# A fused mixer block on one NeuronCore: the six middle blocks of each engine's program become the body of a counted loop

## The reference

```python
mod = silu(c) @ w_ada + b_ada;  shift, scale, gate = split(mod, 3)
h = rms_norm(x, norm_g) * (1 + scale) + shift
proj = h @ w_in                      # 4096 x 1024 @ 1024 x 3592
pool_out = causal_pool_mixer(u) * silu(z_pool)      # windows 2, 4, 8, 16
q, k = silu(causal_depthwise_conv(proj[q, k]))
hm = mlstm_chunkwise(q, k, v, ig, lf)               # chunks of 128, 4 heads, state carried
mlstm_out = rms_norm_heads(hm) * mh_norm_g * sigmoid(o) * silu(z_mlstm)
x = x + gate * (concat(pool_out, mlstm_out) @ w_out)
out = rms_norm(x, final_g)
```

## Time and profile before

| what | value |
|---|---|
| median of 3 runs | 1903.21 us (1901.49 to 1903.31) |
| the profiled execution | 1901.49 us, its span 1899.7 us |
| PE busy | 1815.9 us, 96% of the span, 9505 matmuls |
| DVE busy | 1081.1 us, 57%, 2453 instructions |
| ACT, POOL busy | 470.0 us (25%), 238.1 us (13%) |
| TensorE's granted clock | 0.994 of full speed over the span |
| DMA | 324 MB, 171 GB/s; the 16 DMA engines 51% busy with it |
| code fetched during the run | 1.25 MB in 76 packets (queue 8), 0.35 MB in 43 (queue 14) |

### The profile page before, as it was taken

The page is one execution under the profiler, slowest core; times in us unless marked ns, Lnnn a source line. Parts: engine busy times, 40 slices in busy tenths (PEclk is TensorE's granted clock), DMA queues, the critical chain, the costliest instruction groups (busy, mean ns, idle before and its releaser), DMA issues.

```text
span 1899.7 us, 25000 instructions
## 1 busy us (share of the span) xinstructions
PE 1815.9 (96%) x9505; PEld 1551.8 (82%) x9505; DVE 1081.1 (57%) x2453; ACT 470.0 (25%) x970; POOL 238.1 (13%) x213
## 2 busy tenths in 40 slices
PE   2797999999999999999999999999999999999998
PEld 1686878988888888988889888888889888898886
DVE  7677585454746366372764637544573727636373
ACT  1134432212312122221222122221221212222221
POOL 0443213000120002200030000300012000210000
PEclk9998999999999999999999999999999999999999
DMA  9597952665235652456425663265524564255521
GB/s 298 174 307 261 308 182 78 203 196 200 90 135 191 207 176 80 157 189 210 152 74 186 189 203 119 89 210 189 195 72 164 188 211 150 87 171 193 169 100 67
DMA packets 131483, 324.12 MB, mean 171 GB/s; under 512 B 11724, under 2 KB 49316, under 8 KB 131364
## 3 DMA queue, kind: packets, MB, share of 16 engines
q1 hardware_dynamic: 131364, 322.53, 51.4%
HBM read 276.28 MB, written 46.20 MB: 170 GB/s over the span
## 4 chain that ended last, share of the span: by engine, by line
PE 77%; DVE 11%; DMA 4%; issue 2%; POOL 1%; ACT 1%; SPq 0%; DVEq 0%; POOLq 0%
PE ps_acc L466 21%; PE ps_acc L468 21%; PE ps_acc L467 20%; DMA w_kept<-sb_w_split 3%; DMA sb_w_raw<-w_in 2%; PE ps_kv L466 1%; PE ps_kv L467 1%; PE ps_kv L468 1%; PE ps_num L479 1%; PE ps_sco L625 1%; DVE sb_shifted L1429 1%; DVE sb_acc_cv L1429 1%; PE ps_num L653 1%; PE ps_kv L657 1%; PE ps_num L652 1%
## 5 line engine op out<-in xcount | busy, mean ns | idle before, releaser
L466 PE MATMUL ps_acc<-sb_hT_hi,sb_w_split 128*128 128x512 f32 x1536 | 603.3, 393 | 0.0
L468 PE MATMUL ps_acc<-sb_hT_hi,sb_w_split 128*128 128x512 f32 x1536 | 599.3, 390 | 0.0
L467 PE MATMUL ps_acc<-sb_hT_lo,sb_w_split 128*128 128x512 f32 x1536 | 599.1, 390 | 0.0
L468 PEld LDWEIGHTS ps_acc<-sb_hT_hi,sb_w_split 128*128 128x128 f32 x1536 | 288.8, 188 | 61.4
L467 PEld LDWEIGHTS ps_acc<-sb_hT_lo,sb_w_split 128*128 128x128 f32 x1536 | 289.1, 188 | 59.3
L466 PEld LDWEIGHTS ps_acc<-sb_hT_hi,sb_w_split 128*128 128x128 f32 x1536 | 289.4, 188 | 57.9
L971 POOL TENSOR_TENSOR sb_h_rs<-sb_h_var,sb_mhalf 128x4 f32<-128x4 f32 x32 | 32.4, 1014 | 1118.1 <-DVE sb_h_var L1380 1118.1
L1291 DVE SCALAR_TENSOR_TENSOR sb_acc_cv<-sb_shifted,sb_par,sb_acc_cv 128x512 f32<-128x512 f32 x192 | 146.2, 761 | 6.8
L1314 DVE TENSOR_TENSOR sb_oz<-sb_tanh,sb_oz 128x512 f32<-128x512 f32 x32 | 22.2, 692 | 147.0 <-ACT sb_tanh L855 147.0
L466 PE MATMUL ps_acc<-sb_wo_hi,sb_mixm_hi 128*128 128x512 f32 x256 | 103.9, 406 | 0.0
L468 PE MATMUL ps_acc<-sb_wo_hi,sb_mixm_lo 128*128 128x512 f32 x256 | 100.1, 391 | 0.0
(11 more groups left out here) (220 smaller groups left out, 2884.2 us busy)
## 6 DMA issues: line engine op xcount, KB each, us to landing
sb_w_split<-w_kept SPq DMA_DIRECT2D x344, 512.0 KB, 3.6
sb_w_split<-w_kept SPq DMA_DIRECT2D x56, 520.0 KB, 4.1
w_kept<-sb_w_split SPq DMA_DIRECT2D x40, 512.0 KB, 5.8
sb_x_res<-x SPq DMA_DIRECT2D x34, 512.0 KB, 4.5
out<-sb_x_res SPq DMA_DIRECT2D x32, 512.0 KB, 2.6
sb_x_in<-x SPq DMA_DIRECT2D x30, 512.0 KB, 5.3
sb_w_raw<-w_in SPq DMA_DIRECT2D x48, 256.0 KB, 4.4
w_kept<-sb_w_split SPq DMA_DIRECT2D x8, 520.0 KB, 4.7
```

Source lines behind the costliest of these rows:

```text
L466: pe.matmul(dst, st_hi, mv_hi, start=start, stop=False)
L467: pe.matmul(dst, st_hi, mv_lo, start=False, stop=False)
L468: return pe.matmul(dst, st_lo, mv_hi, start=False, stop=stop)
```

## The change

In each of the five engine functions the Python `for` over blocks 1 to 6 is replaced with a counted loop of the engine (`Fori`). The program of an engine then holds the middle block once; `b` is a register of that engine, each wait whose value hangs on `b` is for the content of a register that the sequencer works out, and the addresses of `x` and `out` are made from `b` too. Blocks 0 and 7 stay as they were, outside the loop. The loops of the five engines are separate, with no barrier at their ends.

```diff
@@ block.sync @@
             one_block(0, False, True)
-            for b in range(1, NB - 1):
+            with sp.Fori(1, NB - 1) as b:
                 one_block(b, False)
             one_block(NB - 1, True)
@@ block.tensor @@
-            for b in range(1, NB - 1):
+            with pe.Fori(1, NB - 1) as b:
@@ block.scalar @@
-            for b in range(1, NB - 1):
+            with act.Fori(1, NB - 1) as b:
@@ block.gpsimd @@
-            for b in range(1, NB - 1):
+            with pool.Fori(1, NB - 1) as b:
@@ block.vector @@
-            for b in range(1, NB - 1):
+            with dve.Fori(1, NB - 1) as b:
```

## The result

| kernel | median | runs | ratio to before |
|---|---|---|---|
| before (measured again beside it) | 1903.26 us | 1900.66 to 1904.02, six | |
| after, five counted loops | 1919.01 us | 1917.57 to 1919.97, six | 1.0085, 95% interval 1.0075 to 1.0096 |

The loops cost 15.8 us, 0.85%. The forecast was slower, 1914 us, 10.6 us for the change: the direction and the range held, the size was a third too small. That the sum was of the right order is largely luck, since its parts were not: in the profiled execution the jumps cost 7.4 us and not 10, and not by the packet of code that the 10 stood for, and the register instructions inside the blocks 6.8 us and not 0.6.

What follows compares the result with a forecast made beforehand. PE's stream was taken to bound every middle block. Jumps at 10 us plus 0.6 us of register work, on 1901.5, gave 1912.1; set 1.7 us higher for the median, 1914 us, own range 1907 to 1921, with rivals 1901 to 1930.

Steps and rivals of the forecast that it cites:

- the register instructions inside the blocks: Register work in the middle blocks: nothing on DVE, 0.1 us at PE's wait of line 479, six times, 0.6 us.
- The period that it named: From the second middle block on, each block would take 226 us, against 223.9 before.
- the second packet: PE code needed ten matmuls past each jump back: there at 7.2 us, PE dry from 5.3; five times, 10 us.
- F: Time to fetch the target's code again at a jump back, taken as 3.6 us, between bounds of 1.2 and 5.1.
- its signs: Expected in the profile: PE idle about 2 us ten matmuls into five blocks; idle at the first matmul means larger F or C.
- The register instruction between two dependent steps: On DVE it runs while the first step is being executed, so it was costed at nothing.
- Rival D: Register work shows on DVE's chain to the head output: 2.7 us a block, 16 us in six, 1919 us; 12%.
- The 0.6 us for PE's own register instruction at line 479: The wait for DVE's head output sits on a sequencer instruction ahead of the matmul: 0.1 us, six times.
- The forecast of 0 for SP, ACT and POOL: Their jumps cost nothing: SP's late load is hidden by PE's own 2.0 us, ACT's fetch lies in its wait, POOL is idle.
- B: The code fetch hides at the jumps and costs PE nothing; 1904 us; 27%.
- C: The sequencer doesn't jump before PE's queue is empty: 6.3 us, five times, 31 us, 1934 us; 10%.
- E: Faster: DVE waits move onto the step itself, 0.6 us a block, 3.8 in six, 1899 us; 6%.

Runs made afterwards that it cites:

- e6: After, with the last load of x_res in each middle block cut to one row of 128; 1914.35 us, ratio to before 1.0053.
- e1: Before, with only PE's six middle blocks made a counted loop; 1905.79 us, ratio to before 1.0011.
- e5: After, but DVE keeps its six copies while SP, ACT, POOL and PE loop; 1907.34 us, ratio to before 1.0021.
- e7: After, but DVE works out all register values of an instruction's waits before stating the first wait; 1908.24 us, ratio to before 1.0029.
- e8: As e7, with register values worked out first on PE, ACT and SP too; 1907.86 us, ratio to before 1.0021.
- e2: Before, with only DVE's middle blocks made a counted loop; 1906.33 us, ratio to before 1.0016.
- e4: After, with two middle blocks in each iteration on all five engines, so two jumps back in place of five; 1912.12 us, ratio to before 1.0049.
- e3: Before, with only SP, ACT and POOL in counted loops; 1903.98 us, ratio to before 1.0003.
- e9: As e8, but PE keeps its six copies; 1904.49 us, ratio to before 1.0004.
- e10: e8 with PE's loop turned to begin behind the first 48 matmuls of a block; 1922.80 us, ratio to before 1.0109.
- e12: e8 with the last seven matmuls of out_p(7) moved from the end to the start of PE's loop body; 1908.57 us, ratio to before 1.0023.

## Why the prediction was right and wrong

**The bound.** That PE's stream bounds every block and that only a break in it or a longer chain into its waits can cost held; the 14.1 us are 11.6 us of such waits and 2.5 in the matmul intervals right beside them. The period that it named, 226 us, was met (226.4 to 226.7, and 225.2 in the sixth block, which has no jump behind it), for other reasons than it gave.

**The jump: the right place, the wrong packet.** PE's code is fetched again, the other engines' jumps cost PE nothing (DVE's stall of 2.7 to 2.9 us lies inside its wait for v, as the prediction said of a fetch there), the jump in is free, and the lead of 4.1 us covers most of the first packet. But all of the 10 us stood for the second packet: 1.9 us of dry PE ten matmuls into a block, since the first packet was held to be just covered. That step was wrong. A second packet starts 3.0 to 4.5 us behind the first at every jump, yet PE was not dry ten matmuls into any block. What cost was the first: F, taken at 3.6 us, has to be set against a branch of 4.6 to 4.9 us with the load of x_res in front and 3.3 to 3.9 without (e6). The prediction's bounds of F, 1.2 and 5.1, held it, and its signs had idle at the first matmul down as a larger F. The term was 10 us and measured 6.1 dry, 7.4 in all, of which some 5 come from DVE's lateness (in all 2.2 in e1, 2.8 in e5, 2.5 in e7, 1.2 in e6). That 10 came near 7.4 is luck.

**Register instructions on DVE: the step that failed.** "The register instruction between two dependent steps runs while the first is being executed" is true for one without a wait and false for one that holds the wait for that very step. The pair that I priced it by the earlier trace rows was of the first kind, and its gap is 0.03 us after the change too; the steps around it are of the second. The order writes those waits beside the register instructions, and I costed these by their 0.05 us against the length of a step instead of asking when they may start. Rival D had the right place, but its condition, a register instruction longer than a step, was the wrong one; its 1919 us is what was measured, by 2.7 us a block on one chain, where the true sum is made of three smaller things. Their sizes: about 1.6 of the 2.0 at line 479, 4.9 at the new wait for x_res, about 5 of the 7.4 at the jumps. e7 takes some 11 us back by moving the waits (and by sharing equal values). The 0.6 us for PE's own register instruction at line 479 was about right: 0.4 in e1, and gone in e8.

**The wait that no part causes alone.** The new wait for x_res was in neither the forecast nor a rival. The accumulator's release (line 1501) starts 209.7 to 210.8 us into a block before, 209.7 to 210.6 in e1, 211.1 to 211.9 in e2 and 212.3 to 212.6 in after. In before it ends 1.0 to 1.8 us ahead of the matmul that needs it, in e2 0.06 to 0.65, and in after PE stands 0.34 to 0.62 us for it in every block (e4 and e6, in which both loop as well, wait too). So DVE's loop alone, with 1.6 us by the middle values, uses up nearly the whole reserve, and what comes on top is paid in full. Of the 2.7 us in after, DVE's loop explains 1.6 and the other four 0.4 (e5); the rest shows only where all are together. The path is the one that DVE's waits hide: out_norm, store, weight load, load of x, ACT's sum of squares, DVE. The load of x goes out 1.8 us later by the middle values, and then takes 5.9 to 6.2 us to land, for 5.0 to 5.9 before.

**SP's jump and the rest.** The forecast of 0 for SP, ACT and POOL held (e3 +0.4, e9 +0.7, both with intervals that hold 1). For SP it held for another reason than the one given: I had counted on a fetch of 3.6 us that PE's own lateness would hide, and there is no such stall, SP's next instruction coming 0.3 us behind its branch. Rivals B, C and E fell: the fetch does not hide on PE, the branch does not wait for PE's queue (the lead of 4.1 us is there at each jump), and nothing became faster.

## What to carry to other kernels

Where a wait's value is in a register, compute all values before stating the first wait; else a register instruction can inherit the wait for the previous step and is then paid in full on a dependent chain. Costs that each fit into a reserve have to be added along the path before they are called free: here the parts cost 5.3 us one at a time and 15.8 together. Before a loop's jump, express the sequencer's lead in instructions and look at which transfer is issued just ahead of it.

## What the runs showed of the hardware that was not expected

- From PE's 47 taken branches in ten kernels: the packet of code starts 2.2 to 2.6 us behind the branch where a 512 KB transfer was issued 0.2 to 0.65 us ahead of it, 1.4 to 2.2 where that was 0.7 to 1.5 us ahead, and 1.0 to 1.4 where it was 1.7 us or more, but for one of 1.8. With the load cut to 4 KB, or issued behind the branch (once 0.1 us ahead), it is 0.9 to 1.5, but for one of 1.7 in e10. The packet takes 0.9 to 1.5 us, the branch ends 1.4 to 1.5 us behind it, and where PE was dry the next matmul started 0.5 to 0.6 us after that with the jump at the block's end, and 0.2 to 0.3 in e10 to e12.
- DVE's taken branch is 0.06 us in the profile and its next instruction comes 2.7 to 3.0 us later: a short branch doesn't say that the jump is free.
- PE's sequencer is 18 matmuls ahead: 4.1 us with matmuls of 0.23 us, 2.2 us with matmuls of 0.12.
- A register instruction on DVE takes 0.04 us and a place of 0.09 us; with the wait for the previous step on it, it adds that to the chain (gaps of 0.20 to 0.22 us for 0.04 with two of them, or one and an EVENT_SEMAPHORE).
- Seven of ten gaps of 2.0 to 2.9 us in PE's full stream were followed by 3.4 us at the lower clock, 1.6 us lost each; none of the gaps of up to 1.7 us in the middle blocks of any kernel here was.
- A gap of PE costs more than itself: 6.1 us dry at five jumps came with 7.4 us between matmul starts, and 3.1 us at six waits with 4.9.
